# Banded attention in a fused two-block kernel: order of the first steps, and how the bias strip is made

## The chip, the cores and the metric

The kernel runs on one core of one Trainium2 chip. The metric is device time in microseconds (us) of that core, one launch of the whole program; the time before is 1220.99 us, the median of 3 runs (1220.89 to 1221.01).

## What is computed

The reference chains two blocks on 512 positions of width 1024, all in float32. The first has a mixer (three branches) and a convolutional feed-forward part; the second has one mixer, banded attention with a per-head sink. Only the second is near the change:

```python
def swa_sink_mixer(xn, w_in, sinks, w_out, t5_table):
    q, k, v, z = jnp.split(xn @ w_in, [nq, nq + nkv, nq + 2 * nkv], axis=-1)
    o = banded_attention(q_heads(q, B, T), kv_heads(k, B, T), kv_heads(v, B, T),
                         t5_table, SWA_WINDOW, sinks)
    return (merge_heads(o, B, T) * jax.nn.silu(z)) @ w_out
# in banded_attention, blocks of 128 queries, each with its own and the preceding 128 keys:
    dist = nprev * Q_BLOCK + jnp.arange(Q_BLOCK)[:, None] - jnp.arange(kc)[None, :]
    valid = (dist >= 0) & (dist < window) & (kpos >= 0)
    bias = jnp.take(t5_table, t5_bucket(dist), axis=0)
    s = jnp.where(valid, s + bias[None, :, :, None], NEG)
    p = jax.nn.softmax(jnp.concatenate([s, sk], axis=-1), axis=-1)[..., :-1]
```

There are 16 query heads, 4 key and value heads of width 64, and a window of 128. `t5_bucket` maps a distance of 0 to 127 to one of 32 rows of the table: 0 to 15 each to a row of their own, larger ones to 16 rows spaced by the logarithm.

## The kernel before

**Products.** Every weight matrix is cut into units of 128 x 1024, 216 of them, four to a round. SyncE (SP) loads a unit into one of four slots of `w_raw` (L405), and waits for that until the unit that was in the slot has been split. ScalarE (ACT) rounds it to `w_high` (L472), VectorE (DVE) subtracts and gets `w_low` (L1225), both two units ahead of TensorE (PE). A product (`product`, L840 to L856) is 24 matmuls of 512 columns: 8 blocks, each high x high, high x low, low x high. PE runs almost only these.

**The bias strip.** The bias of a head depends on the distance alone, so it is kept as a strip of 256 values for each of 16 heads. GpSimd (POOL) waits until the feed-forward part is through (`ffn_low`, L438), loads the table and a one-hot matrix of 32 x 256 (L439, L440) and the two masks of the attention (L441, L442). Between the two halves of the down projection (`down_body(0)` and `down_body(1)`), PE multiplies table and one-hot matrix into 16 x 256 (L1075), and DVE copies the result to `strip` (L1656). POOL stores it to DRAM (L444), copies it there 128 times over (L449, 2 MB), and, when the unit before the round `R_QKV` is through, reads `bias` from it, each partition one value further on (L454, 1 MB). Each of these waits for the transfer before it.

**The attention.** It has 16 steps: 2 pairs of key heads, 4 query blocks, 2 halves; a step treats 4 heads of one block of 128 queries. Steps 0, 1, 8 and 9 belong to the first query block, which has no preceding keys (their score matmuls are 128 columns wide, the others' 256). A step goes through the engines like this:

- PE `scores` (L1118): 4 float32 matmuls, 8 in the trace, into banks 0 and 1 of `side` for an even step, 2 and 3 for an odd one. It waits until DVE has read the scores of the step before last.
- DVE `biased` (L1700 to L1724): picks own or preceding key (L1710), adds the bias and takes the maximum (four times L1717), then the small columns for the softmax (L1721 to L1724). Before L1717 it waits until PE has transposed the step three before, whose buffer it takes.
- ACT `exps` (L764, L766): four exponentials with their sums, and the sink's.
- DVE `normalised` (L1729 to L1733): sum, reciprocal, and the product that PE waits for.
- PE `turn` (L1128): 4 transposes into bank 0 or 1 of `acc`; ACT copies the bank out (`turned_full`, L771), DVE masks it (`masked`, L1747).
- PE `outputs` (L1156) for two steps together, which ACT takes out (L387).

The order on each engine is written out by hand. On PE, with the value rows (`rows`, L886, 24 matmuls of 256 columns for each block of 128 positions) and the eight products of `z`:

```python
            rows(R_QKV + 2, 2, xn, 4, range(1))
            scores(0); scores(1)
            rows(R_QKV + 2, 2, xn, 4, range(1, 3))
            scores(2)
            rows(R_QKV + 2, 2, xn, 4, range(3, 4))
            # for j in 0 to 7:
            #   turn(2j), turn(2j+1), scores(2j+3), scores(2j+4), product of z, outputs(j)
```

On DVE: `biased(0)`, `biased(1)`, `normalised(0)`, `normalised(1)`, `biased(2)`, `normalised(2)`; then in the loop, for each even step, `biased(step + 3)`, the masks, `biased(step + 4)`, at step 0 `v_diff` (L1792), a weight unit (`ahead`, L1225), and last `normalised(step + 3)`, for which `turn(step + 3)` waits. ACT runs `exps(0)` to `exps(2)`, then takes the value rows out of PSUM (L789, four instructions, which release the two banks for the first product of `z`), then `turned_full(0)`, `turned_full(1)`, `exps(3)`, `exps(4)` and a weight unit (`ahead`, L472).

The end is the output product (L1191), the norm in four tiles and their stores.

Of the kernel before, what the change touches and what calls it, by code (L numbers as in the profile page):

```python
# [27 lines left out]
P = 128  # L28
# [69 lines left out]
def build(nc, weights, x, mem, params, consts, table, onehot, rows_g, out):  # L98
    with ExitStack() as ctx:
# [111 lines left out]
        strip = part[0:HEADS_B, 0, 0:2 * P]  # L211
        onehot_sb = convs[0:32, 0, 0:2 * P]
        table_sb = convs[0:32, 0, 2 * P:2 * P + HEADS_B]
# [12 lines left out]
        side = ctx.enter_context(nc.psum_tensor("side", [P, 4, SEQ], F32))  # L226
        strip_dram = nc.dram_tensor("strip_dram", [HEADS_B, 2 * P], F32, kind="Internal")
# [73 lines left out]
        tables_landed = sem("tables_landed")  # L301
        strip_done = sem("strip_done")
        strip_ready = sem("strip_ready")
        strip_stored = sem("strip_stored")
        bias_landed = sem("bias_landed")
# [122 lines left out]
        def _(pool):  # L428
# [20 lines left out]
            pool.dma_start(rows_dram[:, :], bass.AP(strip_dram, 0, [[0, P], [1, row]])).then_inc(strip_stored, 16)  # L449
            pool.wait_ge(strip_stored, 32)  # L450
# [388 lines left out]
        def _(pe):  # L839
# [223 lines left out]
            def down_body(i):  # L1063
# [155 lines left out]
        def _(dve):  # L1219
# [692 lines left out]
```

## Time and profile before

| | value |
|---|---|
| median of 3 runs | 1220.99 us |
| the profiled execution's own time | 1220.97 us |
| its span, first to last instruction | 1219.2 us |
| TensorE's granted clock, mean over the span | 0.999 of full |
| PE busy | 1209.2 us, 99% |
| PE weight loads busy | 1004.5 us, 82% |
| DVE busy | 824.1 us, 68% |
| ACT busy | 491.2 us, 40% |
| POOL busy | 7.5 us, 1% |

The profile is of one execution. Its own time is 1.8 us above its span (what lies before the first and after the last instruction), and within 0.02 us of the median. Times in the rows below are in us from the start of the span, "L" is a line of the kernel, and what stands in square brackets is how long the engine had been idle before the row, with what ended it. `PEld` is TensorE's weight load, which overlaps the matmuls.

### The profile page before, as it was taken

Reading aid. Unit: us, or ns where it says so; the run is one execution under the profiler, and the core shown is the slowest. Engines: PE = TensorE matmul, PEld = TensorE weight load, DVE = VectorE, ACT = ScalarE, POOL = GpSimd, SP = SyncE. Lnnn points to the kernel's source line nnn. Section 1 sums busy time; section 2 is a strip of 40 time slices with the busy share of each in tenths; the row PEclk is TensorE's granted clock in tenths of the full one; section 3 lists DMA queues with packets and bytes.
Section 4 is the critical chain, followed back from the end, with each engine's and each line's share of the span. In section 5 each row is a group of like instructions: output and inputs, shape, how many; then the busy total and the mean of one; then the engine's idle time right before and its main releaser. Section 6 shows DMA issues by size and latency. Waiting matters only on the chain.

```text
span 1219.2 us, 16209 instructions
## 1 busy us (share of the span) xinstructions
PE 1209.2 (99%) x5796; PEld 1004.5 (82%) x5796; DVE 824.1 (68%) x1287; ACT 491.2 (40%) x789; POOL 7.5 (1%) x18
## 2 busy tenths in 40 slices
PE   9999999999999999999999999999999999999998
PEld 8988888888888888888888888888888888887786
DVE  7859797797789987553367866656664443468862
ACT  7643323332333324552244544433443332155643
POOL 0000000000000000000000000000000000000000
PEclk9999999999999999999999999999999999999999
DMA  8523232222222232243322232233223434211211
GB/s 322 175 104 104 81 107 74 84 87 87 69 87 88 101 104 88 85 173 103 103 87 87 93 110 91 86 103 103 101 94 106 172 108 134 96 60 53 80 59 69
DMA packets 35842, 125.53 MB, mean 103 GB/s; under 512 B 4080, under 2 KB 5760, under 8 KB 35536
## 3 DMA queue, kind: packets, MB, share of 16 engines
q1 hardware_dynamic: 33424, 116.41, 28.3%
q0 software_dynamic: 928, 6.08, 1.4%
q10 hardware_dynamic: 1440, 2.36, 0.5%
q8 instruction: 33, 0.54, 0.2%
q14 instruction: 17, 0.14, 0.0%
HBM read 122.72 MB, written 4.21 MB: 104 GB/s over the span
## 4 chain that ended last, share of the span: by engine, by line
PE 96%; DVE 1%; DMA 1%; ACT 1%; issue 0%; SPq 0%; ACTq 0%; DVEq 0%
PE acc L852 79%; PE acc L869 4%; PE side L1191 2%; PE acc L1191 2%; DMA w_raw<-weights 1%; PE acc L1156 1%; PE acc L922 1%; PE acc L941 1%; PE side L941 1%; PE side L991 1%; PE side L1011 1%; PE side L1118 1%; PE acc L1128 1%; PE side L1001 0%; PE side L903 0%; PE side L912 0%
## 5 line engine op out<-in xcount | busy, mean ns | idle before, releaser
L852 PE MATMUL acc<-h_high,w_high 128*128 128x512 f32 x880 | 342.9, 390 | 0.0
L852 PE MATMUL acc<-h_low,w_high 128*128 128x512 f32 x880 | 342.5, 389 | 0.0
L852 PE MATMUL acc<-h_high,w_low 128*128 128x512 f32 x880 | 342.4, 389 | 0.0
L1225 DVE TENSOR_TENSOR w_low<-w_raw,w_high 128x1024 fp32r<-128x1024 f32 x213 | 257.6, 1221 | 43.2 <-ACT w_high L472 39.9
L472 ACT ACTIVATE w_high<-w_raw 128x1024 fp32r<-128x1024 f32 x213 | 221.0, 1051 | 105.4 <-PE acc L852 88.8
L852 PEld LDWEIGHTS acc<-h_high,w_low 128*128 128x128 f32 x880 | 165.1, 188 | 34.6
L852 PEld LDWEIGHTS acc<-h_high,w_high 128*128 128x128 f32 x880 | 165.3, 188 | 34.1
L852 PEld LDWEIGHTS acc<-h_low,w_high 128*128 128x128 f32 x880 | 165.2, 188 | 33.9
L1293 DVE SCALAR_TENSOR_TENSOR convs<-long_u,par,convs 128x510 f32<-128x510 f32 (+28 forms) x232 | 170.3, 734 | 6.6
L852 PE MATMUL acc<-f_high,w_high 128*128 128x512 f32 x176 | 68.6, 390 | 0.0
L852 PE MATMUL acc<-f_low,w_high 128*128 128x512 f32 x176 | 68.5, 389 | 0.0
L852 PE MATMUL acc<-f_high,w_low 128*128 128x512 f32 x176 | 68.5, 389 | 0.0
L852 PE MATMUL acc<-xn_high,w_high 128*128 128x512 f32 x128 | 51.0, 398 | 0.3 <-ACT v L789 0.3
L852 PE MATMUL acc<-xn_high,w_low 128*128 128x512 f32 x128 | 49.9, 390 | 0.0
L852 PE MATMUL acc<-xn_low,w_high 128*128 128x512 f32 x128 | 49.9, 389 | 0.0
L1503 DVE TENSOR_TENSOR gate<-acc,gate 128x512 f32<-128x512 f32 x16 | 11.1, 692 | 55.4 <-PE acc L852 53.9
L1635 DVE TENSOR_TENSOR x<-acc,x 128x512 f32<-128x512 f32 x8 | 5.5, 691 | 54.5 <-PE acc L852 54.5
L852 PEld LDWEIGHTS acc<-f_high,w_high 128*128 128x128 f32 x176 | 33.0, 188 | 7.3 <-issue 0.4
L852 PEld LDWEIGHTS acc<-f_high,w_low 128*128 128x128 f32 x176 | 33.0, 188 | 6.9
L852 PEld LDWEIGHTS acc<-f_low,w_high 128*128 128x128 f32 x176 | 33.0, 188 | 6.7
L635 ACT ACTIVATE ya_high<-part 128x512 fp32r<-128x512 f32 x8 | 5.1, 632 | 71.5 <-DVE part L1478 71.5
L738 ACT ACTIVATE square<-x 128x512 f32<-128x512 f32 x8 | 5.1, 631 | 70.7 <-DVE x L1635 70.7
(330 smaller groups left out, 1865.2 us busy)
## 6 DMA issues: line engine op xcount, KB each, us to landing
w_raw<-weights SPq DMA_DIRECT2D x213, 512.0 KB, 3.2
x_in<-x SPq DMA_DIRECT2D x4, 512.0 KB, 10.0
x<-x POOLq DMA_DIRECT2D x1, 2048.0 KB, 8.6
rows_dram<-strip_dram POOLq DMA_DIRECT2D x1, 2048.0 KB, 12.1
w_raw<-weights SPq DMA_DIRECT2D x4, 384.0 KB, 7.1
mem_in<-mem ACTq DMA_DIRECT2D x4, 256.0 KB, 7.2
bias<-rows_dram POOLq DMA_DIRECT2D x1, 1024.0 KB, 7.2
out<-result ACTq DMA_DIRECT2D x4, 256.0 KB, 2.6
```

Of the source, the lines that this page charges most:

```text
L472: act.activation(w_high[:, s, :], raw[s][:, :], ACT.Copy).then_inc(weight_high, 1)
L852: mm = pe.matmul(acc[:, bank, 0:width], w[:, s, (skip + b) * P:(skip + b + 1) * P], moving[v][:, k, :], start=first and b == 0 and w is w_ ...
L869: mm = pe.matmul(acc[:, s + i, 0:width], w[:, s + i, k * P:(k + 1) * P], moving[v][:, k, :], start=k == 0 and w is w_high and v == 0, stop ...
L922: mm = pe.matmul(acc[:, s, at:at + MEM], w[:, s, k * P:(k + 1) * P], memory[v][:, k, :], start=k == 0 and w is w_high and v == 0, stop=k = ...
L941: mm = pe.matmul(dst, o[:, k, t * P:(t + 1) * P], w[:, s:s + 2, k * P:(k + 1) * P], start=k == 0 and o is mem_high and w is w_high, stop=k ...
L991: mm = pe.matmul(side[:, t // 2, MEM * (t % 2):MEM * (t % 2) + MEM], query[:, 2 * head + d, t * P:(t + 1) * P], key[:, 2 * head + d, :], s ...
L1011: mm = pe.matmul(side[:, d, :], v[:, b, (2 * head + d) * P:(2 * head + d + 1) * P], p, start=b == 0 and i == 0, stop=b == 1 and i == 2)
L1118: mm = pe.matmul(side[:, 2 * (step % 2) + e, MEM * i + P * blocks[0]:MEM * i + MEM], q2[at:at + 64, 4 * p + 2 * half + i, n * P:(n + 1) * ...
L1128: mm = pe.transpose(acc[:, step % 2, r * P:(r + 1) * P], sw_probs[step % 3][:, r, 0:P], ident)
L1191: mm = pe.matmul(bank, o[:, k, t * P:(t + 1) * P], w[:, s, half * SEQ:(half + 1) * SEQ], start=False, stop=k == KT - 1 and o is o2_low)
L1225: dve.tensor_tensor(w_low[:, s, :], raw[s][:, :], w_high[:, s, :].bitcast(F32), ALU.subtract)\
L1293: dve.scalar_tensor_tensor(conv_acc[:, shift:SEQ], long_u[:, tile, 1:SEQ + 1 - shift], w, conv_acc[:, shift:SEQ], ALU.mult, ALU.add).then_ ...
```

## The change

Three things. The strip is no longer computed: POOL writes the strip's rows from the reversed table into DRAM with 17 small transfers, each a run of equal buckets (sources of step 0) or the 16 exact distances, then reads them transposed into `strip_dram`, one value at a time (4096 values), and goes on as before; none of it waits for PE or DVE, and all of it, with the masks, now follows the reload of `x1`. PE's matmul and DVE's copy between the halves of the down projection are gone. And the order of the first steps is changed on PE and DVE, and in the loop `normalised(step + 3)` stands ahead of the weight unit.

```diff
@@ POOL
-            pool.wait_ge(ffn_low, F_TILES)
-            pool.dma_start(table_sb, table).then_inc(tables_landed, 16)
-            pool.dma_start(onehot_sb, onehot).then_inc(tables_landed, 16)
             pool.dma_start(own_keys[:, :], consts[:, 2 * P:3 * P]).then_inc(masks_landed, 16)
             pool.dma_start(older_keys[:, :], consts[:, 3 * P:4 * P]).then_inc(masks_landed, 16)
-            pool.wait_ge(strip_ready, 1)
-            pool.dma_start(strip_dram[:, :], strip).then_inc(strip_stored, 16)
+            runs = bias_runs()
+            for at, row, length, step in runs:
+                pool.dma_start(bass.AP(strip_rows, at * HEADS_B, [[P * HEADS_B, 2], [HEADS_B, length], [1, HEADS_B]]),
+                               bass.AP(table.tensor, row * HEADS_B, [[0, 2], [step, length], [1, HEADS_B]]))\
+                    .then_inc(runs_stored, 16)
+            pool.wait_ge(runs_stored, 16 * len(runs))
+            pool.dma_start(bass.AP(strip_dram, 0, [[2 * P, HEADS_B], [1, 2 * P]]),
+                           bass.AP(strip_rows, 0, [[1, HEADS_B], [HEADS_B, 2 * P]]), allow_slow_non_contiguous=True)\
+                .then_inc(strip_stored, 16)
             pool.wait_ge(strip_stored, 16)
...
@@ PE
-            down_body(0)
-
-            pe.wait_ge(tables_landed, 32)
-            pe.matmul(side[0:HEADS_B, 2, 0:2 * P], table_sb, onehot_sb, start=True, stop=True)\
-              .then_inc(strip_done, 1)
-            down_body(1)
+            for i in range(2):
+                down_body(i)
...
             scores(0)
             scores(1)
-            rows(R_QKV + 2, 2, xn, 4, range(1, 3))
+            rows(R_QKV + 2, 2, xn, 4, range(1, 2))
             scores(2)
-            rows(R_QKV + 2, 2, xn, 4, range(3, 4))
+            scores(3)
+            rows(R_QKV + 2, 2, xn, 4, range(2, 4))
             for j in range(KT):
...
-                for step in (2 * j + 3, 2 * j + 4):
+                for step in (2 * j + 3, 2 * j + 4) if j else (4,):
@@ DVE
-            down_body(0)
-            dve.wait_ge(strip_done, 1)
-            dve.tensor_copy(strip, side[0:HEADS_B, 2, 0:2 * P]).then_inc(strip_ready, 1)
-            down_body(1)
+            for i in range(2):
+                down_body(i)
...
             biased(0)
             biased(1)
+            biased(2)
             normalised(0)
             normalised(1)
-            biased(2)
             normalised(2)
...
                     if step + 4 < 2 * KT:
                         biased(step + 4)
+                    if step + 3 < 2 * KT:
+                        normalised(step + 3)
...
                     ahead(R_Z + step // 8, step // 2 % 4)
-                    if step + 3 < 2 * KT:
-                        normalised(step + 3)
@@ host side: the runs (17 of them), and the table reversed
+    rows = [buckets - 1 - bucket(P - 1 - i) for i in range(P - exact)]
+    starts = [i for i in range(P - exact) if i == 0 or rows[i] != rows[i - 1]]
+    return [(i, rows[i], end - i, 0) for i, end in zip(starts, starts[1:] + [P - exact])] \
+        + [(P - exact, buckets - exact, exact, HEADS_B)]
```

## Rows read from the trace of the kernel before

**Rows 1.** The page, part 1: busy time, share of the span, instructions

```profile
PE 1209.2 (99%) x5796; PEld 1004.5 (82%) x5796; DVE 824.1 (68%) x1287; ACT 491.2 (40%) x789; POOL 7.5 (1%) x18
```

**Rows 2.** The page, part 4: the chain that ended last, by engine

```profile
PE 96%; DVE 1%; DMA 1%; ACT 1%; issue 0%; SPq 0%; ACTq 0%; DVEq 0%
```

**Rows 3.** PE's waits after 1040 us: total, times, longest

```profile
PE acc L1128 <- DVE probs L1733: 1.5, 1, 1.5
```

**Rows 4.** Timeline of PE around the strip: start us, us, engine line op

```profile
950.03 0.39 PE L852 MATMUL acc<-f_high,w_high 128*128 128x512 f32 x1
...
953.20 0.39 PE L852 MATMUL acc<-f_high,w_low 128*128 128x512 f32 x1
953.52 0.60 PE L1075 MATMUL side<-convs 32*16 32x256 f32 x2
...
956.22 0.39 PE L852 MATMUL acc<-f_high,w_high 128*128 128x512 f32 x1
```

**Rows 5.** Timeline of PE, 1082 to 1101 us

```profile
1082.07 1.14 PE L1118 MATMUL side<-k,q 64*128 64x256 f32 x8
1083.14 0.39 PE L886 MATMUL acc<-w_high,xn_high 128*128 128x256 f32 x1
...
1086.12 0.60 PE L1128 MATMUL acc<-ident_sb,probs 128*128 128x128 f32 x4
...
1087.08 2.00 PE L1118 MATMUL side<-k,q 64*128 64x256 f32 x16
1089.35 0.50 PE L852 MATMUL acc<-xn_high,w_high 128*128 128x512 f32 x1 [0.27 <-ACT v L789]
...
1096.04 0.66 PE L1128 MATMUL acc<-ident_sb,gate 128*128 128x128 f32 x4
...
1098.76 2.00 PE L1118 MATMUL side<-k,q 64*128 64x256 f32 x16
1100.69 0.50 PE L852 MATMUL acc<-xn_high,w_high 128*128 128x512 f32 x1
```

**Rows 6.** The same, one iteration later: two transposes without a wait

```profile
1108.23 0.66 PE L1128 MATMUL acc<-ident_sb,sw_probs 128*128 128x128 f32 x4
...
1109.26 1.58 PE L1118 MATMUL side<-k,q 64*128 64x256 f32 x16
```

**Rows 7.** Timeline of DVE, 1079 to 1098 us

```profile
1079.64 0.08 DVE L1717 DVE_READ_ACCUMULATOR2_ANT sw_small<- 128x1 f32 x1
...
1083.90 0.69 DVE L1710 COPY_PREDICATED side<-older_keys,side 128x512 f32<-128x512 int32 x1
...
1092.98 0.95 DVE L1792 TENSOR_TENSOR v_diff<-v 128x768 f32<-128x768 f32 x1
1095.88 1.23 DVE L1225 TENSOR_TENSOR w_low<-w_raw,w_high 128x1024 fp32r<-128x1024 f32 x1 [1.96 <-ACT w_high L472]
...
1097.43 0.69 DVE L1733 TENSOR_TENSOR probs<-probs,small 128x512 f32<-128x512 f32 x1
```

**Rows 8.** Timeline of ACT, 1087 to 1093 us

```profile
1087.77 1.53 ACT L789 ACTIVATE v<-acc,root_col 128x256 f32<-128x256 f32 x4
...
1092.68 0.19 ACT L766 ACTIVATE small<-small 128x4 f32<-128x4 f32 x1
```

**Rows 9.** DMA issues: times, KB each, median us from issue to landing

```profile
rows_dram<-strip_dram POOLq DMA_DIRECT2D x1, 2048.0 KB, 12.1
...
bias<-rows_dram POOLq DMA_DIRECT2D x1, 1024.0 KB, 7.2
...
strip_dram<-part POOLq DMA_DIRECT2D x1, 16.0 KB, 1.7
```

**Rows 10.** Timeline of POOL

```profile
525.67 0.53 POOL L436 DMA_DIRECT2D x<-x  x1 [523.03 <-DVE yb_low L1545]
...
1014.75 1.19 POOL L454 DMA_DIRECT2D bias<-rows_dram  x1 [54.64 <-PE acc L852]
```

**Rows 11.** SP's four weight loads (L405), 955 to 975 us: issue to landing

```profile
DMA to landing us min/median/max: 3.2/6.8/11.7
```

More of the change, by code:

```diff
@@ L95, with build @@
 N_MEM, N_X, N_LN, N_FFN, N_FINAL, N_LAST = range(-2, 4)
-def build(nc, weights, x, mem, params, consts, table, onehot, rows_g, out):
+def build(nc, weights, x, mem, params, consts, table, rows_g, out):
     with ExitStack() as ctx:
@@ L210, in build @@
         ffn_y = [gate[:, 0, :], gate[:, 1, :], conv_acc, conv_sum]
-        strip = part[0:HEADS_B, 0, 0:2 * P]
-        onehot_sb = convs[0:32, 0, 0:2 * P]
-        table_sb = convs[0:32, 0, 2 * P:2 * P + HEADS_B]
         x_sum = part[:, 0, :]
@@ L226, in build @@
         side = ctx.enter_context(nc.psum_tensor("side", [P, 4, SEQ], F32))
+        strip_rows = nc.dram_tensor("strip_rows", [2 * P, HEADS_B], F32, kind="Internal")
         strip_dram = nc.dram_tensor("strip_dram", [HEADS_B, 2 * P], F32, kind="Internal")
@@ L300, in build @@
         ffn_low = sem("ffn_low")
-        tables_landed = sem("tables_landed")
-        strip_done = sem("strip_done")
-        strip_ready = sem("strip_ready")
         strip_stored = sem("strip_stored")
+        runs_stored = sem("runs_stored")
+        rows_stored = sem("rows_stored")
         bias_landed = sem("bias_landed")
@@ L436, in _ @@
             pool.dma_start(x1[:, :, :], x).then_inc(x_again, 16)
-            pool.wait_ge(ffn_low, F_TILES)
-            pool.dma_start(table_sb, table).then_inc(tables_landed, 16)
-            pool.dma_start(onehot_sb, onehot).then_inc(tables_landed, 16)
             pool.dma_start(own_keys[:, :], consts[:, 2 * P:3 * P]).then_inc(masks_landed, 16)
             pool.dma_start(older_keys[:, :], consts[:, 3 * P:4 * P]).then_inc(masks_landed, 16)
-            pool.wait_ge(strip_ready, 1)
-            pool.dma_start(strip_dram[:, :], strip).then_inc(strip_stored, 16)
+            runs = bias_runs()
[7 more added lines that the diff above has]
+                .then_inc(strip_stored, 16)
             pool.wait_ge(strip_stored, 16)
             row = HEADS_B * 2 * P
-            pool.dma_start(rows_dram[:, :], bass.AP(strip_dram, 0, [[0, P], [1, row]])).then_inc(strip_stored, 16)
-            pool.wait_ge(strip_stored, 32)
+            pool.dma_start(rows_dram[:, :], bass.AP(strip_dram, 0, [[0, P], [1, row]])).then_inc(rows_stored, 16)
+            pool.wait_ge(rows_stored, 16)
             toeplitz = bass.AP(rows_dram, P - 1, [[row - 1, P], [2 * P, HEADS_B], [1, P]])
@@ L1820, in _, with bias_runs, bucket @@
                                          g_last_rows[:, SEQ:D], ALU.mult, ALU.mult).then_inc(result_ready, 1)
-def distance_columns():
+def bias_runs():
     import numpy as np
     exact, buckets, far = 16, 32, 128
-    picks = np.zeros((buckets, 2 * P), np.float32)
-    for i in range(2 * P):
-        dist = (P - 1 - i) % WINDOW
-        large = exact + int(np.float32(np.log(max(dist, 1) / exact)) / np.log(far / exact) * (buckets - exact)) \
-            if dist >= exact else 0
-        picks[dist if dist < exact else min(large, buckets - 1), i] = 1.0
-    return picks
+    def bucket(dist):
+        if dist < exact:
+            return dist
+        large = exact + int(np.float32(np.log(dist / exact)) / np.log(far / exact) * (buckets - exact))
+        return min(large, buckets - 1)
+    rows = [buckets - 1 - bucket(P - 1 - i) for i in range(P - exact)]
+    starts = [i for i in range(P - exact) if i == 0 or rows[i] != rows[i - 1]]
+    return [(i, rows[i], end - i, 0) for i, end in zip(starts, starts[1:] + [P - exact])] \
+        + [(P - exact, buckets - exact, exact, HEADS_B)]
 def kernel(**inputs):
@@ L1899 @@
                                   np.triu(np.ones((P, P), np.float32)), np.triu(np.ones((P, P), np.float32), 1)], 1),
-        "table": np.ascontiguousarray(a["t5_table_2"]),
-        "onehot": distance_columns(),
+        "table": np.ascontiguousarray(a["t5_table_2"][::-1]),
         "rows_g": np.ascontiguousarray(a["final_g_2"]).reshape(1, D),
```

## The prediction

> **What bounds the kernel now.** I read the page first. PE is busy 1209.2 us of a span of 1219.2 [rows 1], and the chain of work that ended last is 96% PE [rows 2]; DVE, at 824.1 us, and ACT are far from full. So a change pays only by what it takes out of PE's own stream: an instruction of PE, or a gap in it. What DVE, ACT, POOL or a transfer does beside that is worth nothing until PE waits for it. The second view is therefore PE's waits. After 1040 us there are two: 1.5 us at a transpose, for DVE's normalisation (L1733) [rows 3], and 0.27 at the first product of `z`, for ACT's evictions of the value rows (L789) [rows 5]. The third view is the timeline of PE, to see what the strip's matmul costs and what each stretch takes when nothing waits.
>
> **The strip's matmul, removed.** Starts of L852 show its price, since matmuls overlap. From 950.03 to 953.20 there are 14 steps, 0.2264 us each. From 953.20 to 956.22 there are 10 steps of L852 with the strip's matmul (two entries of the trace) inside; ten plain steps would be 2.26, and the rows show 3.02 [rows 4]. The price is 0.76, more than its own 0.60 us, as the matmuls behind it start a little late. No semaphore held PE there, so all of it is saved. I take 0.75, with 0.6 (its own length) and 0.9 as ends.
>
> The Trainium skill has a rule that would give less (TensorE: Matmul & The Clock Gate, Single matmul latency): a lone matmul at full clock takes about (398 + N) / 2.4 ns, which is an estimate of 0.27 us for 256 columns, and 0.38 with a second pass of 256 columns behind it. By that the time would come out at 1218.6 instead of 1218.2. The page states it for bf16 alone, and the rows of this float32 matmul decide.
>
> **DVE's copy of the strip** (L1656) goes too. DVE has no part in the chain there, so I cost it at nothing.
>
> **The wait at the transpose of step 3.** `turn(2)` starts at 1096.04 and the scores behind `turn(3)` at 1098.76, 2.72 us later; one iteration on, two transposes without a wait take 1109.26 - 1108.23 = 1.03 [rows 5, 6]. So the wait is worth 1.69 in PE's stream, a little over the 1.5 of [rows 3]. Its cause is the order on DVE. After `biased(4)` come `v_diff` at 1092.98, a wait of 1.96 for ACT's rounding of a weight unit, `w_low` at 1095.88, and only then the normalisation, whose last instruction runs from 1097.43 to 1098.12 [rows 7]. With the normalisation ahead of the first two, it could start at 1092.98: ACT's last exponential of step 3 ends at 1092.68 + 0.19 = 1092.87 [rows 8]. It takes about 1.0 (the small sum, the reciprocal, 0.69), so it is ready at 1094.0, while PE asks for `turn(3)` half of 1.03 after 1096.04, at 1096.55. That is 2.5 us to spare with this one edit. `scores(3)` moved ahead adds to it. DVE can then begin `biased(3)` straight after `normalised(2)` and waits only for `turn(0)`. Queued behind that new wait are `biased(4)` and the normalisation, and they are still some 2 us earlier than before. I take the whole 1.69; its ends are 1.0 (a third of it comes back as another wait) and 1.7.
>
> **What is late next on DVE** is `v_diff` and `w_low`, each one normalisation (1.0 us) later than it would be. `v_diff` is first read by `outputs(1)`, beyond the second product of `z`, over 10 us on; `w_low` is two units ahead, over 10 us too. Both are covered. In all later iterations the same swap holds; PE doesn't wait there now, so it saves nothing and has the same cover.
>
> **The wait at the first product of `z`.** Two sets of scores take 1.93 when nothing waits (1098.76 to 1100.69), and took 2.27 before that product (1087.08 to 1089.35) [rows 5]: 0.34 lost. The evictions start at 1087.77 and take 1.53 [rows 8], though the value rows were through by 1086.3: ACT was at `exps(2)`, because DVE reached step 2 only at 1083.90, behind two normalisations [rows 7]. Now `scores(2)` follows one block of value rows instead of two. A block is half of what lies between the pairs of scores, about 2.9 us, so `scores(2)` starts near 1079.2, and DVE can take it at 1080.4, 3.5 us earlier than 1083.90, with the normalisations behind it. `exps(2)` ends near 1084.6 instead of 1087.8.
>
> But the cover gets shorter too, and this is the term I am least sure of. Scores alone cost 1083.14 - 1082.07 = 1.07 and a second set behind them 1.93 - 1.07 = 0.86 [rows 5]. With `scores(3)` moved ahead of the last value rows, these end 0.86 later, at about 1087.15. Then ACT needs 1.53 and perhaps 0.1 to start: 1088.75 to 1088.8. PE meanwhile does `turn(0)` and `turn(1)` (1087.08 - 1086.12 = 0.96) from 1086.98, and `scores(4)` alone (1.07): it asks for the banks at 1089.01 [rows 5]. That leaves 0.2 us. I take the whole 0.34, with 0 as its other end.
>
> **Scores moved.** No score matmul is added, and there are as many changes between scores and other matmuls as before, so PE's own work stays as it is. `scores(3)` needs DVE to have read step 1, which it has at 1079.64 + 0.08 = 1079.72 [rows 7], while PE comes to it at 1080.1. `turn(0)` needs `normalised(0)`. DVE does `biased(2)` from 1080.4 to 1082.5 and then the two normalisations, done by 1084.6, with 2.4 us left to 1086.98.
>
> **The transfers.** On POOL's queue, after `x1` at 525.67 [rows 10], come 2 masks, 17 runs and the transposed read, 20 more issues at about 0.5 each: until 536. The transposed read moves 4096 single values, which no row shows. From below, 16 KB landed in 1.7 us; by pieces, `bias` (2048 pieces) took 7.2, 3.5 ns each, which gives 14 us; `rows_dram` (128 pieces of 16 KB) took 12.1, 95 ns each, which gives 387 us [rows 9]. I take 14, as the bias read is nearest in number of pieces. Even with 387 the copy of 2 MB would be through by about 940, and the read of `bias` isn't due before 1014.75 [rows 10]. So the chain of transfers is hidden. Its other effect is on the weight loads. Beside the copy of 2 MB a load took up to 11.7 us instead of 3.2 [rows 11], and PE had no wait. A slot comes round in four units, 4 x 24 x 0.2264 = 21.7 us, of which about 2.3 are its splitting: a load has 19 us. Cost nothing, ends 0 and the rival below.
>
> **The sum.** 0.75 + 1.69 + 0.34 = 2.78. The profiled execution's 1220.97 (1219.2 of span and 1.8 around it) becomes 1218.19; the median of the runs shown is 0.02 above it. I predict 1218.2.
>
> **Rivals.**
> (a) *The eviction wait stays.* The 0.2 us of slack is within what PE's modelled ends can hide. Against it speaks only that sum. It leaves 2.44: 1218.5, just where it counts as a gain.
> (b) *The transpose's wait comes back elsewhere*: DVE's new wait for `turn(0)` inside `biased(3)` delays `biased(4)`, and so `exps(4)`, the next weight unit or the scores behind it. The work is ordered more tightly at the start, but DVE is idle for 2 us and more in that stretch [rows 7]. It would leave the strip's 0.75 and a third of the rest: 1219.5.
> (c) *Slower: the single-value transfer starves the weight loads.* It runs in the stretch behind 537 us, beside one load in 5.4 us. It decides once a load lands over 19 us after its issue for ACT, and some 30 us for PE, which has two split units in hand. A load held back 40 us would cost 40 - 30 = 10 us: 1228. The load stretched to 11.7 beside a far larger transfer speaks against it [rows 11]. The skill speaks for it (DMA: Bandwidth & Descriptors, Rules for kernel authors): a strided last dimension becomes one descriptor per element and should be rearranged; no row here shows such a transfer.
> (d) *More than the sum*: a gap that the page books as matmul time closes as well, 1217.7.
>
> **How the numbers follow.** About 0.2%, 2.4 us, is what a measurement of this kernel can tell from no change. The forecast has 0.64, (a) 0.14, (b) 0.12, (c) 0.04, (d) 0.06. The bounds of the terms give 1218.0 (0.9 + 1.7 + 0.34) for the most. Towards the least, 0.6 + 1.0 + 0 gives 1219.4, but not all terms are at their ends together; the range stops at 1219.2 and leaves out most of (b) and (c). Below it reaches to 1217.7. A gain over 0.2% means below 1218.55: the forecast nearly whole, (a) partly, (d). That makes 0.68 faster, 0.28 the same, 0.04 slower.
>
> **What would show it.** No entry of L1075 between the halves, and L852 going on at 0.2264. In PE's waits no transpose waiting for L1733 and no product for L789. The normalisation of step 3 ahead of `v_diff`, ended 2 us or more before `turn(3)`. Weight loads near 540 us landing under 12 us, and no wait of ACT for `w_raw`. The prediction is wrong if PE shows a wait at another line of the first two iterations, if the matmuls around the seam keep a gap, or if a weight load behind 537 us lands late.

## The result, and the profile after

The changed kernel takes 1223.95 us (median of 18 runs, 1221.88 to 1225.43), and the kernel before, run in turn with it, 1220.99 us (18 runs, 1220.87 to 1221.14). The ratio is 1.0024, with an interval of 1.0018 to 1.003: slower by a quarter of a per cent, where the prediction said 1218.2 and at most 1219.2. The profiled execution took 1222.08 us, with a span of 1220.3; it is the second fastest of the 18 and 1.9 us under the median, so it shows less than the median run lost. The span before was 1219.2. Lines have moved a little: product L855 (was L852), scores L1117 (L1118), turn L1127 (L1128), normalisation L1731 (L1733), value rows out L792 (L789), weight loads L402 (L405), ACT's split L475 (L472), the bias add L1715 (L1717). DVE's split is L1225 in both.

The page, parts 1 and 4 (by engine), answers to [rows 1, 2]:

```profile
PE 1210.0 (99%) x5794; PEld 1006.0 (82%) x5794; DVE 824.1 (68%) x1286; ACT 491.1 (40%) x789; POOL 17.2 (1%) x33
...
PE 95%; DMA 3%; DVE 1%; ACT 0%; issue 0%; SPq 0%; ACTq 0%; DVEq 0%
```

PE has lost the strip's two entries and is nevertheless busy 0.8 us longer. In the chain of work DMA has 3% of it, some 36 us, where it had 1%. The first thing to ask is where PE waits for it. PE's waits over the whole span (what waited, for what, total, times, longest):

```profile
PE acc L855 <- DVE w_low L1225: 2.0, 1, 2.0
PE acc L925 <- DVE mem_low L1313: 1.7, 1, 1.7
PE side L953 <- POOL convs L426: 1.3, 1, 1.3
```

Both waits that the change aimed at are gone: the 1.5 at the transpose [rows 3] and the 0.27 at the product of `z` [rows 5]. The last two rows here belong to the kernel's start and stand in the profile of before too. The first is new: PE stood still for a weight unit that DVE had not split. Its place is far from the attention, in the timeline of PE:

```profile
575.90 0.39 PE L855 MATMUL acc<-yb_high,w_low 128*128 128x512 f32 x1
578.25 0.63 PE L855 MATMUL acc<-h_high,w_high 128*128 128x512 f32 x1 [1.95 <-DVE w_low L1225]
578.68 0.63 PE L855 MATMUL acc<-h_low,w_high 128*128 128x512 f32 x1
...
581.67 0.49 PE L855 MATMUL acc<-h_high,w_low 128*128 128x512 f32 x1
582.00 0.39 PE L855 MATMUL acc<-h_high,w_high 128*128 128x512 f32 x1
```

Two losses lie here. The stop: the matmul at 578.25 was due at 575.90 + 0.23 = 576.13, so 2.12 us. And behind it nine matmuls up to 582.00 start 0.43 us apart instead of 0.23: 3.75 us where nine plain steps are 9 x 0.2264 = 2.04, so 1.71 us. That is the granted clock, in the windows before, at and behind the stop (us from and to, length; busy time and count of PE, PEld, DVE, ACT, POOL; granted clock, DMA share, GB/s):

```profile
541.00:575.00 34.00, 34.00 (x152) 28.16 (x150) 11.13 (x16) 7.07 (x9) 1.55 (x2) 1.00 0.70 40
575.00:578.20 3.20, 1.29 (x6) 0.75 (x4) 1.23 (x1) 1.10 (x2) 0.53 (x1) 1.00 0.69 174
578.20:582.00 3.80, 3.75 (x9) 2.94 (x10) 2.52 (x4) 1.59 (x2) 0.00 (x0) 0.55 1.05 442
582.00:586.00 4.00, 4.00 (x19) 3.32 (x18) 3.06 (x4) 2.81 (x4) 0.00 (x0) 1.00 1.02 388
```

The third row is the stretch behind the stop: 0.55 of full, nearly the lower level of 1.2 GHz, and 1.00 again from 582.00. Together 3.83 us. With the predicted 2.78 taken off, the span should be 1219.2 - 2.78 + 3.83 = 1220.25, and 1220.3 is what it is.

The first of these windows also names the culprit. The same window of the kernel before:

```profile
541.00:575.00 34.00, 34.00 (x152) 28.16 (x151) 13.49 (x18) 9.66 (x12) 0.00 (x0) 1.00 0.32 103
```

PE works alike in both, but ACT runs 9 instructions instead of 12, and the DMA engines are busier (0.70 against 0.32) while they move 40 GB/s instead of 103. POOL's timeline says what began at 541 and ended before 575:

```profile
527.27 9.66 POOL L441 DMA_DIRECT2D strip_rows<-table  x17
540.93 1.61 POOL L445 DMA_DIRECT2D strip_dram<-strip_rows  x1 [4.00 <-DMA strip_rows<-table]
574.99 0.53 POOL L452 DMA_DIRECT2D rows_dram<-strip_dram  x1 [32.45 <-DMA strip_dram<-strip_rows]
```

The transfer of 4096 single values, 16 KB, took 32.45 us behind its issue (the prediction took 14). Beside it SP issues two weight loads, at 548.8 and 550.0 us. From issue to landing, the load issued at 538.7, just ahead of the transfer, and the one issued at 550.0:

```profile
DMA to landing us min/median/max: 4.5/4.5/4.5
...
DMA to landing us min/median/max: 28.2/28.2/28.2
```

In the kernel before, the loads issued at 548.8 and 549.9 landed 3.3 and 4.6 us later. ACT waits for these loads; waits of ACT from 520 to 620 us, and its timeline at the first of the two:

```profile
ACT w_high L475 <- DMA w_raw<-weights: 7.6, 2, 6.4
```

```profile
575.88 1.06 ACT L475 ACTIVATE w_high<-w_raw 128x1024 fp32r<-128x1024 f32 x1 [6.38 <-DMA w_raw<-weights]
```

The unit for which PE stops is that of the load issued at 548.8. The profile has no landing for it, but ACT could take it up at 575.88, 27.1 us behind its issue; ACT and DVE needed 2.3 us more for the split, and PE wanted it at 576.13: there is the stop. The load that took 28.2 us is the next one, and its unit was ready in time.

Nothing is wrong at the attention. The timeline of PE there, which answers to [rows 5]:

```profile
1078.14 1.16 PE L1117 MATMUL side<-k,q 64*128 64x128 f32 x16
...
1091.05 1.14 PE L1117 MATMUL side<-k,q 64*128 64x256 f32 x8
1092.11 0.50 PE L855 MATMUL acc<-xn_high,w_high 128*128 128x512 f32 x1
...
1098.79 0.66 PE L1127 MATMUL acc<-ident_sb,gate 128*128 128x128 f32 x4
1099.29 0.60 PE L1127 MATMUL acc<-ident_sb,probs 128*128 128x128 f32 x4
1099.82 2.00 PE L1117 MATMUL side<-k,q 64*128 64x256 f32 x16
```

`turn(2)` and `turn(3)` take 1099.82 - 1098.79 = 1.03 us, as without a wait [rows 6], and the single set of scores 1.06. The pair of scores that starts at 1098.76 in [rows 5] starts 1.06 us later here, but the scores at the stretch's beginning start 3.11 us later (1078.14), so the order has saved 3.11 - 1.06 = 2.05 us; predicted were 1.69 + 0.34 = 2.03. The scores at the beginning, in the kernel before:

```profile
1075.03 1.16 PE L1118 MATMUL side<-k,q 64*128 64x128 f32 x16
```

DVE's timeline of the changed kernel shows how:

```profile
1090.83 0.29 DVE L1715 CUSTOM_DVE_ANT_0 probs<-side,bias 128x128 f32<-128x128 f32 x1 [1.50 <-PE acc L1127]
...
1094.94 0.69 DVE L1731 TENSOR_TENSOR probs<-probs,small 128x512 f32<-128x512 f32 x1
```

The new wait for `turn(0)` is there (1.50), and the normalisation, now ahead of `v_diff` at 1095.55 and the split at 1097.18, ends at 1095.63, 3.7 us before `turn(3)` starts.

### The profile page after: what moved, and what is told of

It is laid out like the page before. It is cut to its first block, busy times and chain, and to the rows that moved or that the text cites. A ratio compares the mean times of both kernels' runs of the same rounds, so it can differ in the third digit from the quotient of the medians.

```text
span 1220.3 us, 16219 instructions
## 1 busy us (share of the span) xinstructions
PE 1210.0 (99%) x5794; PEld 1006.0 (82%) x5794; DVE 824.1 (68%) x1286; ACT 491.1 (40%) x789; POOL 17.2 (1%) x33
## 3 DMA queue, kind: packets, MB, share of 16 engines
q1 hardware_dynamic: 33424, 116.41, 29.5%
## 4 chain that ended last, share of the span: by engine, by line
PE 95%; DMA 3%; DVE 1%; ACT 0%; issue 0%; SPq 0%; ACTq 0%; DVEq 0%
PE acc L855 77%; PE acc L872 4%; DMA w_raw<-weights 3%; PE side L1191 2%; PE acc L1191 2%; PE side L1117 1%; PE acc L1155 1%; PE acc L889 1%; PE acc L925 1%; PE acc L944 1%; PE side L944 1%; PE side L994 1%; PE side L1014 1%; PE acc L1127 1%; DVE w_low L1225 0%; PE side L1004 0%
## 5 line engine op out<-in xcount | busy, mean ns | idle before, releaser
L855 PE MATMUL acc<-h_high,w_high 128*128 128x512 f32 x880 | 344.0, 391 | 2.0 <-DVE w_low L1225 2.0
L855 PE MATMUL acc<-h_low,w_high 128*128 128x512 f32 x880 | 343.6, 390 | 0.0
L855 PE MATMUL acc<-h_high,w_low 128*128 128x512 f32 x880 | 343.4, 390 | 0.0
L1225 DVE TENSOR_TENSOR w_low<-w_raw,w_high 128x1024 fp32r<-128x1024 f32 x213 | 257.8, 1221 | 49.0 <-ACT w_high L475 45.6
L475 ACT ACTIVATE w_high<-w_raw 128x1024 fp32r<-128x1024 f32 x213 | 221.1, 1051 | 112.2 <-PE acc L855 88.1
L855 PEld LDWEIGHTS acc<-h_high,w_high 128*128 128x128 f32 x880 | 165.7, 188 | 36.5 <-DVE w_low L1225 2.4
L855 PEld LDWEIGHTS acc<-h_high,w_low 128*128 128x128 f32 x880 | 165.7, 188 | 34.3
L855 PEld LDWEIGHTS acc<-h_low,w_high 128*128 128x128 f32 x880 | 165.7, 188 | 34.1
L855 PE MATMUL acc<-f_low,w_high 128*128 128x512 f32 x176 | 68.5, 389 | 0.0
L855 PE MATMUL acc<-f_high,w_low 128*128 128x512 f32 x176 | 68.5, 389 | 0.0
L855 PE MATMUL acc<-f_high,w_high 128*128 128x512 f32 x176 | 68.5, 389 | 0.0
L855 PE MATMUL acc<-xn_high,w_high 128*128 128x512 f32 x128 | 51.1, 399 | 0.0
L855 PE MATMUL acc<-xn_high,w_low 128*128 128x512 f32 x128 | 49.9, 390 | 0.0
L855 PE MATMUL acc<-xn_low,w_high 128*128 128x512 f32 x128 | 49.9, 390 | 0.0
L855 PEld LDWEIGHTS acc<-f_high,w_high 128*128 128x128 f32 x176 | 33.1, 188 | 6.9
L855 PEld LDWEIGHTS acc<-f_low,w_high 128*128 128x128 f32 x176 | 33.1, 188 | 6.9
L855 PEld LDWEIGHTS acc<-f_high,w_low 128*128 128x128 f32 x176 | 33.1, 188 | 6.7
L501 ACT ACTIVATE gate<-acc,par 128x512 f32<-128x512 f32 x24 | 16.4, 685 | 43.3 <-PE acc L855 37.6
```

The lines of the kernel that those rows point to most:

```text
L475: act.activation(w_high[:, s, :], raw[s][:, :], ACT.Copy).then_inc(weight_high, 1)
L501: act.activation(gate[:, half, :], acc[:, 2 * half, :], ACT.Sigmoid, bias=0.0 if bias_col is None else bias_col).then_inc(taken[2 * half], 1)
L855: mm = pe.matmul(acc[:, bank, 0:width], w[:, s, (skip + b) * P:(skip + b + 1) * P], moving[v][:, k, :], start=first and b == 0 and w is w_ ...
L1225: dve.tensor_tensor(w_low[:, s, :], raw[s][:, :], w_high[:, s, :].bitcast(F32), ALU.subtract)\
```

## The experiments

Three chips took part: A (the first four kernels), B (the next four), C (the last four). The kernel before was measured again on each: 1221.05, 1221.00 and 1221.09 us. Ratios are against that. On which chip the first measurement ran is not on record.

### First: which part costs, which part pays (chip A)

Theory T: the 4096 single values cost all of it, through the weight loads. Rival R: the order of the attention, or the 17 runs and masks, costs part of it.

**e1_contiguous.** The transposed read becomes one contiguous copy; this leaves the strip's transposition out.

```diff
-            pool.dma_start(bass.AP(strip_dram, 0, [[2 * P, HEADS_B], [1, 2 * P]]),
-                           bass.AP(strip_rows, 0, [[1, HEADS_B], [HEADS_B, 2 * P]]), allow_slow_non_contiguous=True)\
+            pool.dma_start(strip_dram[:, :], bass.AP(strip_rows, 0, [[2 * P, HEADS_B], [1, 2 * P]]))\
```

> The changed kernel with one transfer exchanged: strip_dram is filled from strip_rows by a contiguous copy of the same 16 KB instead of the read of 4096 single values. It leaves out the transposition of the strip, so the bias is another one; every other instruction stays. Theory T (the transfer of single values keeps the weight loads from landing, PE stops for its weights and then runs for some us at half clock): no such stop, 1218.2 (1220.97 - 0.75 - 1.69 - 0.34), and a spread of a few tenths as before. Rival S (the burst of 17 small transfers with the masks and x1 in front of it, or the copy of 2 MB moved into this stretch): still 1222 to 1224. Rival O (the new order costs somewhere): above 1218.2 by what it costs.

Measured: 1218.23 us (1218.15 to 1218.51), ratio 0.9977 (0.9967 to 0.9986). POOL's timeline: the same 16 KB are through 1.99 us behind their issue.

```profile
541.15 0.53 POOL L445 DMA_DIRECT2D strip_dram<-strip_rows  x1 [4.34 <-DMA strip_rows<-table]
543.67 0.53 POOL L451 DMA_DIRECT2D rows_dram<-strip_dram  x1 [1.99 <-DMA strip_dram<-strip_rows]
```

The predicted 1218.2 is there as soon as the single values are gone. The 17 runs, the masks and the copy of 2 MB cost nothing.

**e2_order.** The kernel before with the new order alone, as in the diff of the change (PE and DVE parts of the attention).

```diff
-            rows(R_QKV + 2, 2, xn, 4, range(1, 3))
+            rows(R_QKV + 2, 2, xn, 4, range(1, 2))
             scores(2)
-            rows(R_QKV + 2, 2, xn, 4, range(3, 4))
+            scores(3)
+            rows(R_QKV + 2, 2, xn, 4, range(2, 4))
```

> The kernel before with the new order alone (scores of steps 2 and 3, biased(2) ahead, normalisation ahead of the weight unit); strip by PE's matmul as before. T and S: 1220.97 - 1.69 - 0.34 = 1218.9 to 1219.0. O: 1221 or more.

Measured: 1219.02 us (1218.90 to 1219.20), ratio 0.9983 (0.9974 to 0.9993): 2.03 us less than before, the two wait terms together (that it fits to the hundredth is luck: the runs spread over 0.3). Between e2 and e1 lie 0.79 us, the strip's matmul (taken: 0.75).

**e3_transfers.** The changed kernel with the old order, the reverse of the diff above and of DVE's.

> The changed kernel with the old order: the strip by transfers alone is all that changes against before. T and S: 1223.95 + 2.03 = about 1226, spread over some 3 us. O: about 1221.

Measured: 1220.89 us (1220.32 to 1222.27), ratio 0.9998 (0.9989 to 1.0008). T had 1226, and missed. The profiled execution, 1220.45 us, is within 0.2 of the kernel before less the 0.75 of the matmul. Eight of the other nine runs are at 1220.8 or more, up to 1222.27, and what they lost no profile shows. POOL's timeline, and the loads issued from 538 to 552 us:

```profile
572.44 0.53 POOL L452 DMA_DIRECT2D rows_dram<-strip_dram  x1 [29.46 <-DMA strip_dram<-strip_rows]
```

```profile
DMA to landing us min/median/max: 3.9/14.3/24.3
```

The transfer was 3.0 us shorter than in the changed kernel, no load took longer than 24.3 us, and PE had no stop there. Either the cost was not in the transfer, or it starts only above some length, and this chip lay below it.

**e4_half.** Half of the single values: the strip's second half repeats its first, so it can be copied from it in 16 pieces of 512 B.

```diff
-            pool.dma_start(bass.AP(strip_dram, 0, [[2 * P, HEADS_B], [1, 2 * P]]),
-                           bass.AP(strip_rows, 0, [[1, HEADS_B], [HEADS_B, 2 * P]]), allow_slow_non_contiguous=True)\
+            pool.dma_start(bass.AP(strip_dram, 0, [[2 * P, HEADS_B], [1, P]]),
+                           bass.AP(strip_rows, 0, [[1, HEADS_B], [HEADS_B, P]]), allow_slow_non_contiguous=True)\
                 .then_inc(strip_stored, 16)
             pool.wait_ge(strip_stored, 16)
+            pool.dma_start(strip_dram[:, P:2 * P], strip_dram[:, 0:P]).then_inc(strip_stored, 16)
+            pool.wait_ge(strip_stored, 32)
```

> The changed kernel, same result, with half as many single values: the first 128 columns of the strip are read transposed (2048 values), the second 128 are a copy of them in 16 pieces of 512 B. Theory T: at 33 us for 4096 values the transfer takes about 16 us, less than the 19 us that a weight load has, so PE never stops: 1218.2 with a spread of tenths. If what costs is having single values in the queue at all: half of the 5.7 us, 1221. S: 1222 to 1224 unchanged.

Measured: 1218.30 us (1218.11 to 1219.64), ratio 0.9978 (0.9969 to 0.9988), and no load over 18.6 us (one run of the ten took 1219.64, at a mean clock of 0.998, so even here the edge may be touched). But half the values took far more than half the time (POOL's timeline):

```profile
564.25 0.51 POOL L449 DMA_DIRECT2D strip_dram<-strip_dram  x1 [22.32 <-DMA strip_dram<-strip_rows]
```

### Second: is there a threshold, and where (chip B)

**e5_again.** The changed kernel, unedited.

> The changed kernel itself, unedited, beside three others on the same chip. The run with the old order was 1220.89, 0.65 over the 1220.24 that it would be without any stop, where 1226 was expected. Theory K (the cost has a kink: PE stops only when a weight load lands later than about 25 us after its issue; the transfer of single values takes 29 to 33 us and its length differs from chip to chip or from run to run): here between 1218.8 and 1225.5, and the profile's load landing, its stop of PE and its time go together: landing below 25 us with no stop and about 1218.5, 28 us with 2 us of stop, 1.7 of half clock and 1222. Rival N (new order and transfer together cost something that neither has alone): 1223 to 1225 whatever the landing says.

Measured: 1218.92 us (1218.09 to 1219.67), ratio 0.9983 (0.9974 to 0.9992). On this chip the same kernel is a gain of 2.1 us. Its profile has a transfer of 29.75 us, loads that land up to 25.8 us after issue, and a stop of a quarter of a microsecond. PE's timeline:

```profile
576.00 0.39 PE L855 MATMUL acc<-yb_high,w_low 128*128 128x512 f32 x1
576.65 0.50 PE L855 MATMUL acc<-h_high,w_high 128*128 128x512 f32 x1 [0.26 <-DVE w_low L1225]
```

**e6_more.** 2048 further single values, to a tensor that nothing reads; 6144 in all.

```diff
+            pool.dma_start(bass.AP(strip_more, 0, [[P, HEADS_B], [1, P]]),
+                           bass.AP(strip_rows, 0, [[1, HEADS_B], [HEADS_B, P]]), allow_slow_non_contiguous=True)\
+                .then_inc(more_stored, 16)
             pool.wait_ge(strip_stored, 16)
+            pool.wait_ge(more_stored, 16)
```

> The changed kernel with a second transfer of 2048 single values right behind the first, into a scratch tensor: 6144 in all, same result. K: the transfer lasts 10 to 16 us longer, all of it beyond the kink, so PE stops for 10 us or more and then runs at half clock for some us: 1230 to 1240. If the cost is a fixed one of any such transfer: 1224 to 1227.

Measured: 1232.67 us (two runs, 1232.29 and 1233.04), ratio 1.0095 (1.0077 to 1.0114). POOL's timeline, then PE's:

```profile
541.48 1.61 POOL L447 DMA_DIRECT2D strip_dram<-strip_rows  x1 [4.53 <-DMA strip_rows<-table]
...
586.37 0.53 POOL L458 DMA_DIRECT2D rows_dram<-strip_dram  x1 [42.23 <-DMA strip_more<-strip_rows]
```

```profile
575.90 0.39 PE L861 MATMUL acc<-yb_high,w_low 128*128 128x512 f32 x1
588.87 0.79 PE L861 MATMUL acc<-h_high,w_high 128*128 128x512 f32 x1 [12.58 <-DVE w_low L1231]
...
592.87 0.48 PE L861 MATMUL acc<-h_high,w_high 128*128 128x512 f32 x1
```

With the stop at the same unit, made only by more single values, the cause is shown: the order of the attention is as in e5. From the end of the first issue, as in the other kernels, the single values take 42.23 + 1.05 = 43.3 us. Against e5's profiled execution, 14.1 us more: 12.3 of stop and about 2 of half clock behind it (nine matmuls from 588.87 to 592.87 take 4.00 us instead of 2.04).

**e7_paced.** The 4096 values in four transfers of 1024, one behind each of the rounds that follow, so that no load should be held up for long.

```diff
+            for part_of in range(4):
+                at = 64 * part_of
+                pool.wait_ge(unit_done, 4 * (R_OUT + 1 + part_of))
+                pool.dma_start(bass.AP(strip_dram, at, [[2 * P, HEADS_B], [1, 64]]),
+                               bass.AP(strip_rows, HEADS_B * at, [[1, HEADS_B], [HEADS_B, 64]]),
+                               allow_slow_non_contiguous=True).then_inc(strip_stored, 16)
+                pool.wait_ge(strip_stored, 16 * (part_of + 1))
```

> The changed kernel, same result, with the 4096 single values in four transfers of 1024, the first behind the first round of the output projection and each 21.8 us after the one before (POOL waits for the unit count). K: each part takes 8 to 12 us, no load lands later than about 15 us, PE never stops: 1218.2. If the number of single values is what costs, wherever they are: as the unedited change beside it.

Measured: 1222.97 us (1220.00 to 1225.89, one run of 1738 apart), ratio 1.0016 (1.0006 to 1.0027). A miss. A quarter of the values takes about 20 us, not 8 (POOL's timeline; the last of the four was issued at 702.74):

```profile
722.66 0.53 POOL L455 DMA_DIRECT2D rows_dram<-strip_dram  x1 [19.15 <-DMA strip_dram<-strip_rows]
```

How long the first three took is not seen, as POOL waits for a round behind them. The loads issued in the stretches of the four took up to 20.2, 22.0, 12.6 and 21.3 us, so most of some 90 us had late loads, instead of 30. And from 631 to 652 us, beside the first, the DMA queues (packets, MB, share of the 16 engines' time) look like this:

```profile
q1 hardware_dynamic: 185, 0.71, 78.0%
...
q0 software_dynamic: 32, 0.00, 0.8%
```

Here the time is booked on the weights' own packets (q1) and hardly on POOL's queue (q0). That is not so in every profile: from 541 to 575 us q1 has 52.2% and q0 16.6% in the changed kernel, and q1 26.7% and q0 63.0% in e6. Everywhere the weights' packets are few and long, but whether they wait behind the single values or are slow themselves, these bookings don't tell. PE's stop, 2.8 us at 655.28, is at the first product of the feed-forward part's rounds (L875), which begins with two units at once; that it therefore has less lead is argued, not measured. Behind this stop too the matmuls start 0.43 us apart, for six steps.

**e8_layout.** No transposition at all, and the transposed read is left out: the bias stays position by head in SBUF, and the copies are contiguous (128 rows of 8 KB in the last).

```diff
-            toeplitz = bass.AP(rows_dram, P - 1, [[row - 1, P], [2 * P, HEADS_B], [1, P]])
+            toeplitz = bass.AP(rows_dram, (P - 1) * HEADS_B, [[row - HEADS_B, P], [1, P * HEADS_B]])
...
-bias[:, head, :], 1.0, NEG,
+bias[:, :, head], 1.0, NEG,
```

> The changed kernel, same result, without any transfer of single values: the rows are copied 128 times as they are (position by head), and bias is kept as 128 positions x 16 heads, read in pieces of 8 KB; DVE's bias operand in L1715 then has a step of 16 elements. K: 1218.2. If DVE reads such an operand slower, its 64 instructions of 0.29 us get longer; at twice that the chain of the first steps is 1.2 us a step later and the wait at the first transposes comes back: 1219 to 1221.

Measured: 1218.55 us (1218.47 to 1218.93), ratio 0.998 (0.9971 to 0.9989). The transfer's cost is gone on this chip too, but DVE reads the bias with a step of 16 values. First the bias add in e8, then in the changed kernel (min/median/max in ns):

```profile
L1709 DVE CUSTOM_DVE_ANT_0 probs<-side,bias x24: 357/367/384, 1075.9 to 1149.9; 128x128 f32<-128x128 f32 x24
```

```profile
L1715 DVE CUSTOM_DVE_ANT_0 probs<-side,bias x24: 285/286/292, 1079.8 to 1153.2; 128x128 f32<-128x128 f32 x24
```

That is 0.08 us per instruction, 0.32 a step. It matters once: the pair of scores behind the second block of value rows waits until step 1 has been read, and takes 2.35 us instead of 2.00. That is e8's distance of 0.3 to e1 and e4. The Trainium skill puts a price on such steps (Vector Engine (DVE) Microarchitecture Reference, Measured stream behaviour on trn2): about 0.65 cycle per element on a port that hops to another region at every element, measured with hops of 4 KiB, and more for small steps. At the page's 0.96 GHz that is an estimate of 0.68 ns. The step here is 64 B, and the trace has 0.081 us over 128 elements, 0.63 ns each: about the price of the long hops, and not more.

### Third: what about the single values, and the two halves of the order (chip C)

**e9_again.** The changed kernel again, as the neighbour of e10.

> The changed kernel, unedited, a third time. It was 1223.95 first and 1218.92 beside e6 to e8; the load behind the transfer landed 28.2 us after its issue in the first profile, 25.8 in the second. Theory K (kink at about 25 us, the rest is the length of the transfer): any time between 1218.2 and 1225.5, but in step with the landing and PE's stop in its own profile. Rival N (a cost that the transfer alone doesn't explain): a time that doesn't go with the landing.

Measured: 1223.81 us (1221.35 to 1224.71), ratio 1.0021 (1.0012 to 1.003): slower again, as in the first measurement. Its profile caught the fastest of its runs, 1221.35, with a transfer of 32.43 us:

```profile
575.71 0.39 PE L855 MATMUL acc<-yb_high,w_low 128*128 128x512 f32 x1
579.08 0.50 PE L855 MATMUL acc<-h_high,w_high 128*128 128x512 f32 x1 [2.98 <-DVE w_low L1225]
579.41 0.40 PE L855 MATMUL acc<-h_low,w_high 128*128 128x512 f32 x1
```

A stop of 3.1 us, longer than in the first measurement, and no half clock behind it. The mean granted clock of the runs separates the two: the two runs at 1.000 took 1221.35 and 1221.48, the nine at 0.996 to 0.998 took 1222.83 to 1224.71. So the stop is worth 3.1 us here; that the clock behind it costs 2.4 more in the median run is an estimate, which takes the stop as equal in all of them. In the first measurement the picture is less clean: 1221.88 at 1.000, and 0.996 only at 1224.5 and more, but two runs at 0.999 took 1224.58 and 1224.62, so there the stop itself was probably longer in some runs.

**e10_sbuf.** The same single values, but written into rows of the two mask tiles in SBUF, and from there to DRAM in pieces of 512 B; the masks are loaded after.

```diff
+            for half, tile in enumerate((own_keys, older_keys)):
+                pool.dma_start(tile[0:HEADS_B, :], bass.AP(strip_rows, half * P * HEADS_B, [[1, HEADS_B], [HEADS_B, P]]),
+                               allow_slow_non_contiguous=True).then_inc(strip_stored, 16)
+            pool.wait_ge(strip_stored, 32)
+            for half, tile in enumerate((own_keys, older_keys)):
+                pool.dma_start(strip_dram[:, half * P:(half + 1) * P], tile[0:HEADS_B, :]).then_inc(strip_stored, 16)
+            pool.wait_ge(strip_stored, 64)
```

> The changed kernel, same result, with the 4096 single values read into SBUF (16 rows of the two mask tiles, 2048 each) and stored from there as 32 pieces of 512 B; the masks are loaded behind that. It takes the single-value writes to DRAM away and leaves the single-value reads. If the writes are what holds the weight loads up: the transfer is over in under 15 us, no load lands later than 12 us, 1218.2. If the reads are: a transfer of 25 us or more, and a time like that of the unedited change beside it.

Measured: 1218.29 us (1218.14 to 1218.60), ratio 0.9977 (0.9968 to 0.9986), beside 1223.81 for e9 on the same chip. POOL's timeline:

```profile
540.86 1.07 POOL L442 DMA_DIRECT2D own_keys<-strip_rows  x1 [4.94 <-DMA strip_rows<-table]
541.92 1.04 POOL L442 DMA_DIRECT2D older_keys<-strip_rows  x1
548.28 0.51 POOL L446 DMA_DIRECT2D strip_dram<-own_keys  x1 [5.32 <-DMA older_keys<-strip_rows]
```

The weight loads issued from 538 to 552 us:

```profile
DMA to landing us min/median/max: 3.3/4.3/4.6
```

4096 reads of single values from DRAM into SBUF are through 7.4 us after the first issue, at 548.3, and the next weight load is issued only then: they hold nothing up here, and whether a longer such read would, no run shows. What costs 30 us is single values with DRAM as their destination. No run writes single values from SBUF to DRAM, so it could also be that source and destination are both DRAM. The Trainium skill has a line that fits (DMA: Bandwidth & Descriptors, Specifications): below 512 B the DMA engine reads, modifies and writes back. The runs agree as far as they go: 512 B pieces to DRAM (e4, e10) are quick, 4 B pieces are not; but the 17 runs also write rows below 512 B, 256 of 64 B, and cost nothing (e1). Whether that mechanism is the reason no run here shows.

**e11_swap** and **e12_start** split the order: e11 is the kernel before with the normalisation ahead of `v_diff` and the weight unit in DVE's loop; e12 the kernel before with `scores(3)` and `biased(2)` early.

```diff
 # e11: DVE's loop
+                    if step + 3 < 2 * KT:
+                        normalised(step + 3)
                     if step == 0:
 # e12: ahead of DVE's loop, and PE's order as in e2
+            biased(2)
             normalised(0)
             normalised(1)
-            biased(2)
```

> The kernel before with one edit: in DVE's loop the normalisation stands ahead of v_diff and the weight unit. By the rows of before it is ready 2.5 us ahead of turn(3), so the whole 1.69 goes and the 0.34 of the eviction stays: 1219.3. If the DVE reaches it no earlier (a rival in which ACT's exponentials are what is late): 1220.5 or more.

> The kernel before with the other edit of the order: scores(3) ahead of the last value rows and biased(2) ahead of the first normalisations, on PE and DVE; the loop of DVE as before. The 0.34 goes, and as biased(3) and biased(4) come some 2 us earlier, the normalisation behind the weight unit is ready at about 1096.4, near 1096.2 where PE asks for it: 1219.0 to 1219.4. If the two edits were worth only their own waits: 1220.6.

Measured: e11 1219.53 us (1219.17 to 1219.80), ratio 0.9987 (0.9978 to 0.9996), with the wait of 0.3 for the value rows left; e12 1219.22 us (1219.07 to 1219.45), ratio 0.9985 (0.9976 to 0.9994), with neither wait left. Alone they save 1.56 and 1.87, together 2.03 (on chip A): the first wait needs only one of them, the second only the early start.

## Why the prediction was wrong

**The strip's matmul, 0.75: right.** e1 less e2 gives 0.79, and in the changed profile L855 goes on at 0.2264 across the seam.

**The wait at the transpose, 1.69, and the wait at the product of `z`, 0.34: right.** 2.05 from the two timelines, 2.03 from e2. Also the term of which I was least sure: the evictions end at 1091.9 and the product starts at 1092.11, the 0.2 us of slack that the sum had. The prediction thought of the swap as sufficient for the transpose, and it is (e11), but so is the early start (e12). The rivals (a), (b) and (d) did not come about: e1, e4 and e10 stand at 1218.23 to 1218.30, and their profiles show none of the attention's waits of PE.

**The transfers, "Cost nothing": wrong, and this is the step that failed.** In the profiled execution they cost 3.83 us, in the median run 1223.95 - 1218.2 = 5.75. The step had three parts.

First the size: "I take 14, as the bias read is nearest in number of pieces". It was 32.45 us. The bounds of 1.7 and 387 held it, but the row that I took as nearest was a transfer into SBUF in pieces of 512 B. Nearest in number was not nearest in kind: e10 moves 4096 single values into SBUF in 7.4 us, twice as fast as I took, so it is the destination, DRAM in pieces of 4 B, that no row of before showed. By number of values the time is 20 us for 1024 (e7), 22.3 for 2048, 29.5 to 32.5 for 4096 and 43.3 for 6144, so that no price per value could have given it.

Second the effect on others. I asked only how long the transfer takes and leaned on [rows 11], where a load beside 2 MB took 11.7. A transfer of 16 KB held loads back to 28.2 us: what it moves says nothing of what it holds up.

Third the margin. "A load has 19 us", and "some 30 us for PE": rival (c) named the place and the mechanism, and only its edge was off. The rows of the runs:

| run | transfer, us | landing of the load whose unit PE needs at 576, us behind its issue | wait of PE, us |
|---|---|---|---|
| e4_half (A) | 22.3 | 18.4 | none |
| e3_transfers (A) | 29.5 | 24.3 | none |
| e5_again (B) | 29.8 | 25.3 | 0.3 |
| changed kernel | 32.5 | 27.1 (until ACT begins) | 2.0 |
| e9_again (C) | 32.4 | 28.0 | 3.0 |
| e6_more (B) | 43.3 | 37.6 | 12.6 |

Up to 25 us a late load costs nothing; beyond, a microsecond for each (12.6 - 0.3 = 12.3 of waiting for 37.6 - 25.3 = 12.3 of landing). The profile of before holds this edge. There ACT takes this unit up at its usual time, 19.1 us behind the issue at 548.8:

```profile
567.85 1.99 ACT L472 ACTIVATE w_high<-w_raw 128x1024 fp32r<-128x1024 f32 x2
```

It is split 2.3 us later, at 570.1, and PE wants it at 576.1. So the 19 us of the prediction were right, and PE had 6 us in hand, about one unit of 24 x 0.2264 = 5.43: 19.1 + 6 = 25. The prediction counted two units, and so came to 30. With 14 or 387 as the only sizes, that edge looked far off. A chance of 0.04 was too little for a price that was known only between 1.7 and 387 us, with an edge at 30 inside.

**Not in the sum at all: the clock behind a stop.** 1.71 us in the profiled execution, an estimated 2.4 in the median run of e9. The runs at a mean clock of 1.000 are 0.3 (e9) to 0.9 us (first measurement) above the kernel before, so the stop alone eats up the gain of 2.78, and the clock makes most of the loss.

The median run was not profiled. As a rough estimate, 1223.95 is made up like this: 1218.2 as predicted, some 3.7 us of stop (1221.88, the run at 1.000, less 1218.2) and some 2.1 of half clock; the two profiled stops are 2.1 and 3.1.

**What stays open** is why the same transfer takes 29.5 to 29.8 us on chips A and B and 32.4 us on C, and so makes a gain of 2.1 us or a loss of 2.7. No run here changes this. Nor do the runs show why the clock falls behind a stop of 2.1 us in one execution and not behind 3.1 in another, or by what the single values slow the weights' packets.

**The versions that beat both.** e10_sbuf (1218.29 on the chip where the changed kernel takes 1223.81) and e4_half (1218.30). I would take e10: its loads issued beside the single values land within 4.6 us, far from the edge of 25, while e4's 18.4 is 7 us from it. Each has run on one chip only.

## What to carry to other kernels

Before a transfer goes beside a stream of loads, look at the size of its pieces on the DRAM side when it writes, not at its bytes: single values are transposed on the way into SBUF, and go to DRAM in rows. State the lead of the loads in microseconds, and when a price is known only between bounds that have the edge between them, give the case beyond the edge a real chance. A stop of PE of 2 us can cost 4, because the clock may fall behind it; and with an edge so near, a gain on one chip is a loss on the next, so measure on more than one.

## What the runs showed of the hardware that I had not expected

- Copying 4096 single values from DRAM to DRAM takes 29.5 to 32.5 us, 1024 still about 20 (19.15 for the last of four, e7); moving 4096 from DRAM into SBUF takes 7.4 (e10).
- During such copies the weights on another queue come slowly: all queues together move 40 GB/s in the changed kernel from 541 to 575 us, where they moved 103 before, and 34 in e7 from 631 to 652. The time is booked on the weights' packets in e7 (78.0% against 0.8%), on POOL's in e6 (26.7% against 63.0%).
- The granted clock fell to about half behind stops of 2.1 us (changed kernel, nine matmuls), 2.8 (e7, six) and 12.6 (e6, nine), and did not behind one of 3.1 (e9).
- The same kernel, 1218.92, 1223.81 and 1223.95 in three measurements, while the medians of the one before stayed within 0.1 us of 1221.0.
- A float32 operand of DVE read with a step of 16 values costs 0.367 instead of 0.286 us for 128 elements per partition.
